# Setup of a two-layer mixer kernel: token tiles loaded first, scaled in pairs and turned row by row, zero products added, context work moved

## The chip, the cores and the metric

One core of one Trainium2 chip (trn2) runs the kernel, all in fp32. The metric is the device time of one execution in microseconds (us). The engines are TensorE (PE), VectorE (DVE), ScalarE (ACT), GpSimd (POOL) and SyncE (SP), which issues most DMAs. Before the change the median of 3 runs is 1315.41 us (1314.79 to 1315.99).

## The reference, cut to what matters

512 tokens `x` and 256 context rows `ctx` of 1024 features go through a first block (two gated linear-attention mixers) and then two attention layers. The change lies in the very first steps of the first block:

```python
mod_x = jnp.matmul(jax.nn.silu(c), w_mod[l]) + b_mod[l]
mod_c = jnp.matmul(jax.nn.silu(c_ctx), w_mod[l]) + b_mod[l]
...
hx = rmsnorm(x, norm_g[l]) * (1.0 + sc_x[:, None, :]) + sh_x[:, None, :]
hc = rmsnorm(ctx, norm_g[l]) * (1.0 + sc_c) + sh_c
z = jnp.matmul(h, w_in)        # queries, keys, values, gates, low-rank gate inputs
```

The relative-position bias (`rel_bias_2` against a one-hot table) is also turned into rows in the setup; the attention layers read them from DRAM much later.

## The kernel before

Each engine has one in-order program, written as functions `setup_t` (TensorE), `setup_v` (VectorE), `setup_a` (ACT), `setup_g` (POOL), `setup_s` (SP), followed by `gla_t`, `gla_v` and so on. There is no planner: the order on every engine is the order of the code, and engines meet through counting semaphores (`nt`, `nv`, `na`, `ng` hold the counts, `s_...` those of landings). `meet(e, "setup")` at the head of the `gla_*` functions waits for every engine's setup and for the bias rows' landing in DRAM (`s_br`).

The setup has these pieces. Tiles 2 to 5 of `xsv` are the tokens (128 rows of 1024 each), tiles 0 and 1 the context.

- SP (L294 to L314) issues in order: `c`, `c_ctx`, the identity (`cst`), 4 token tiles, 2 context tiles, two parts of `w_mod` (k = 0 and 2), the low-rank weights, the first half of the query and key weights (`s_aq`), then `w_mod` 1 and 3, the rest of the query weights, the constants, the weights of `load(s, 2)`, and, once ACT has written the bias rows, three stores to `bias_rows`. ACT's own queue (L485 to L489) loads small rows, `gdn_conv`, `rel_bias` and the one-hot table.
- ACT waits for `c` and `c_ctx`, does the silu (L492), then the squares with row sums of the six tiles in the order 2, 3, 4, 5, 0, 1 (L495). It later copies the bias rows and half of the turned tiles out of PSUM.
- VectorE copies `vec`, `cvec` and `rt` (L421 to L426) out of PSUM, makes the roots' arguments (`rsq_v`, L407), for which POOL takes the power of -0.5 (`rsq_g`, L412), and scales the tiles (L458, L462): all four token tiles after one root.
- TensorE turns the small rows (L320 to L324), makes the bias rows (`brow`, products of 33 rows by 13 columns), turns the tokens feature block by feature block, four row tiles each, so all four scaled tiles are needed for the first one (L353), does `mod(0)`, turns the context (L362), does `mod(2)`, and turns the two product rows into columns (`mod_turned`, products with 2 columns). `mod(k)` is 512 columns of the modulation matrix; from parts 0 and 2 come shift and scale of features 0 to 511 (`turned`, L443 to L446), from 1 and 3 those of features 512 to 1023.
- VectorE and ACT modulate the turned tiles in place in SBUF, `hT` for tokens, `hC` for context (L451, L453, L512, L514), the even ones on VectorE and the odd ones on ACT.
- TensorE then does `low_rank(t, 0)` on the first four feature tiles, and `mod(1)`, `mod(3)` and parts of the query products (`queries`) in turn. `gla_t` goes on with `low_rank(t, 1)`, `queries(t, 0, 4, 8)`, the products with `gla_up` (loaded at L601, after the meeting), `queries(t, 1, 4, 8)` and the keys (`key(0)`, `key(1)`). Nearly all products have line L147 (`mm`). An fp32 product is issued as two passes, so 8 of the trace's MATMULs of 512 columns are 4 products.

The products of the later stages wait for features through `t.wait_ge(...)` by parity of the tile; PSUM banks are handed out by `ps.take` from a ring or by number.

## Time and profile before

| | us |
|---|---|
| median of 3 runs | 1315.41 |
| profiled execution, span of its instructions | 1313.0 |
| what lies around the span, median less span | 2.4 |
| TensorE busy in the span | 1266.9 |
| VectorE / ACT / POOL busy | 698.7 / 417.0 / 398.1 |

How to read it: the span runs from the first instruction of the program to the last, of one execution that the profiler recorded; the time of the runs has a fixed part more, ahead and behind. The trace's times count from the span's start. An engine's busy time says how full it is over the whole span; what a change of one stage is worth has to be read from that stage.

### The profile page before, as it was taken

How to read it: one execution, taken by the hardware profiler on the slowest of the kernel's cores; microseconds unless marked ns; L12 is line 12 of the kernel's file. 1: busy time of each engine (PE TensorE's matmuls, PEld its weight loads, DVE VectorE, ACT ScalarE, POOL GpSimd, SP SyncE). 2: the span in 40 equal slices, each digit the busy share in tenths (PEclk: the TensorE clock that was granted, in tenths of full speed). 3: DMA queues.
4: the chain of work that ended last, by engine and by line, in shares of the span. 5: the costliest groups of instructions: out<-in, count | busy, mean ns of one | idle time of the engine just before them, and what ended most of it. 6: DMA issues, size and time to landing. Idle time of an engine off the chain costs nothing.

```text
span 1313.0 us, 24617 instructions
## 1 busy us (share of the span) xinstructions
PE 1266.9 (96%) x9971; PEld 772.5 (59%) x9971; DVE 698.7 (53%) x1422; ACT 417.0 (32%) x904; POOL 398.1 (30%) x470
## 2 busy tenths in 40 slices
PE   5999999999999999999999999999999999999997
PEld 3454655555656666687445885446645786455553
DVE  4356567847234444573473563247646373237745
ACT  4243213253433332101024002347613102236721
POOL 0100000202334443181432320225761250115671
PEclk9999999999999999999999999999999999999999
DMA  9710112011130100042426315110004415100001
GB/s 308 288 64 0 67 66 80 26 39 65 66 130 3 67 3 3 2 153 104 147 74 137 97 32 192 65 53 1 2 16 98 135 33 192 65 1 2 1 1 64
DMA packets 71535, 96.59 MB, mean 74 GB/s; under 512 B 27639, under 2 KB 35247, under 8 KB 71422
## 3 DMA queue, kind: packets, MB, share of 16 engines
q1 hardware_dynamic: 71050, 94.76, 21.7%
q8 instruction: 78, 1.28, 0.4%
q14 instruction: 35, 0.29, 0.1%
q10 hardware_dynamic: 372, 0.27, 0.1%
HBM read 92.89 MB, written 2.13 MB: 72 GB/s over the span
## 4 chain that ended last, share of the span: by engine, by line
PE 85%; DVE 6%; SPq 3%; ACT 3%; issue 1%; DMA 1%; POOL 0%; DVEq 0%; POOLq 0%; ACTq 0%
PE PS L147 81%; PE PS L2830 2%; DVE AR L2936 2%; ACT AR L3058 1%; SPq L187 1%; DMA bias_rows<-AR 1%; DVE AR L2923 1%; SPq L304 1%; SPq L308 1%; ACT AR L3068 0%; SPq L309 0%; SPq L312 0%; DVE AR L2106 0%; DVE AR L866 0%; PE PS L2164 0%
## 5 line engine op out<-in xcount | busy, mean ns | idle before, releaser
L147 PE MATMUL PS<-AR 64*64 64x64 f32 (+13 forms) x9334 | 1196.2, 326 | 21.8 <-ACT AR L3068 6.0
L147 PEld LDWEIGHTS PS<-AR 64*64 64x64 f32 (+5 forms) x9334 | 703.0, 152 | 485.1 <-issue 384.7
L3058 ACT ACTIVATE AR<-AR 128x257 f32<-128x257 f32 (+5 forms) x160 | 84.9, 531 | 96.1 <-DVE AR L2936 86.1
L2936 DVE CUSTOM_DVE_ANT_0 AR<-PS,AR 128x257 f32<-128x257 f32 (+5 forms) x160 | 72.2, 451 | 60.5 <-PE PS L147 43.0
L412 POOL TENSOR_TENSOR AR<-AR 128x1 f32<-128x1 f32 (+4 forms) x26 | 21.9, 841 | 258.6 <-DVE AR L407 211.8
L1189 DVE SCALAR_TENSOR_TENSOR AR<-AR 128x441 f32<-128x441 f32 (+2 forms) x96 | 78.6, 819 | 15.7 <-ACT AR L1146 12.0
L3119 POOL TENSOR_SCALAR AR<-AR 128x257 f32<-128x257 f32 (+5 forms) x96 | 53.4, 556 | 75.8 <-DVE AR L2942 70.3
L1612 DVE TENSOR_TENSOR AR<-PS,AR 128x256 f32<-128x256 f32 x60 | 25.5, 424 | 85.7 <-PE PS L147 82.4
L3117 POOL TENSOR_SCALAR AR<-AR 128x128 f32<-128x128 f32 (+3 forms) x64 | 39.0, 609 | 68.4 <-DVE AR L2942 64.5
L2053 POOL TENSOR_TENSOR AR<-AR 128x512 f32<-128x512 f32 x36 | 49.6, 1377 | 29.0 <-DMA AR<-in_w_o 26.0
L1738 ACT ACTIVATE AR<-PS 128x512 f32<-128x512 f32 x48 | 28.7, 597 | 82.5 <-PE PS L147 80.3
L2830 PE MATMUL PS<-AR 128*128 128x128 f32 x352 | 49.0, 278 | 4.5 <-DVE AR L2923 3.8
L2830 PEld LDWEIGHTS PS<-AR 128*128 128x128 f32 x352 | 38.6, 141 | 23.7 <-issue 12.4
L2106 DVE TENSOR_TENSOR AR<-PS,AR 128x512 f32<-128x512 f32 x40 | 27.7, 691 | 45.1 <-PE PS L147 43.3
L2372 POOL TENSOR_TENSOR AR<-AR 128x512 f32<-128x512 f32 x32 | 39.7, 1242 | 16.8 <-PE PS L147 13.9
L1850 POOL TENSOR_TENSOR AR<-AR 128x512 f32<-128x512 f32 x20 | 21.0, 1050 | 71.0 <-PE PS L147 62.4
L3068 ACT ACTIVATE AR<-PS 128x512 f32<-128x512 f32 (+2 forms) x56 | 30.0, 536 | 28.6 <-PE PS L2830 24.5
L2573 DVE SCALAR_TENSOR_TENSOR AR<-AR,PS 128x512 f32<-128x512 f32 x16 | 11.0, 687 | 52.0 <-ACT AR L2578 52.0
L2398 DVE SCALAR_TENSOR_TENSOR AR<-PS,AR 128x256 f32<-128x256 f32 x56 | 23.8, 424 | 25.8 <-PE PS L147 15.8
L3129 POOL TENSOR_TENSOR AR<-AR 128x28 f32<-128x28 f32 (+3 forms) x8 | 2.5, 315 | 99.9 <-DVE AR L2952 99.3
L1209 POOL TENSOR_TENSOR AR<-AR 128x512 f32<-128x512 f32 (+1 forms) x12 | 13.0, 1082 | 64.6 <-ACT AR L1155 46.4
L2923 DVE COPY AR<-PS 128x512 f32<-128x512 f32 (+2 forms) x48 | 28.9, 602 | 6.5 <-PE PS L2830 4.7
(264 smaller groups left out, 964.8 us busy)
## 6 DMA issues: line engine op xcount, KB each, us to landing
AR<-in_w_in SPq DMA_DIRECT2D x16, 2048.0 KB, 9.1
AR<-in_w_mod SPq DMA_DIRECT2D x6, 2048.0 KB, 13.1
AR<-in_w_out SPq DMA_DIRECT2D x4, 2048.0 KB, 13.0
AR<-in_x SPq DMA_DIRECT2D x8, 512.0 KB, 5.1
AR<-in_w_in SPq DMA_DIRECT2D x4, 1024.0 KB, 7.4
AR<-in_w_o SPq DMA_DIRECT2D x2, 2048.0 KB, 8.2
AR<-in_w_in SPq DMA_DIRECT2D x2, 1664.0 KB, 8.7
AR<-in_w_in SPq DMA_DIRECT2D x12, 256.0 KB, 4.2
```

The costliest lines, as they stand in the source:

```text
L147: return t.matmul(o, l, r, start=s, stop=p, skip_group_check=True)
L1189: v.do.scalar_tensor_tensor(out=o_, in0=xi[:, r0 + i - 1:r1 + i - 1, c0 + c - 1:c1 + c - 1], scalar=tap(i, c), in1=o_, op0=ALU.mult, op1=A ...
L1738: a_.do.activation(XX[n], ps.two("xx", n, k_, k)[:, new_at(k):new_at(k) + 512], ACT.Copy, bias=0.0, scale=1.0).then_inc(sa, na("xx", n, k_ ...
L2053: g.do.tensor_tensor(o, x, y, ALU.subtract).then_inc(sg, ng(*name, "T"))
L2372: g.do.tensor_tensor(o, x, y, op).then_inc(sg, ng("lS", l, p, i))
L2830: x = t.go.transpose(p[:, c + 128 * b:c + 128 * b + 128], PB[j % NJP][e][:, at[b]:at[b] + 128], ident)
L2923: write(dst, src).then_inc(sem, count("pT", l, j, e))
L2936: v.do.tensor_tensor_reduce(PB[j % NJP][e][:, 0:nk], ps["s", l, j, e][:, 0:nk], bias_for(qb, kind, 2 * a + e, nk), 1.0, 3e38, ALU.add, ALU ...
L3058: a_.do.activation(P, P, ACT.Exp, bias=mn[:, j % NJS, e:e + 1], scale=-1.0, accum_out=su[:, j % NJS, e:e + 1]).then_inc(sa, na("p", l, j, e))
L3068: out_of_psum(a_, sa, na, lambda o, x: a_.do.activation(o, x, ACT.Copy, bias=0.0, scale=1.0), l, i - TURN, e)
L3117: x = g.do.tensor_scalar(P, P, r, gt_[:, qb, c:c + 1], ALU.mult, ALU.mult)
L3119: x = g.do.tensor_scalar(P, P, r, one_c, ALU.mult, ALU.mult)
```

## The change

SP loads the token tiles ahead of `c`, `c_ctx` and the identity. POOL first clears a spare region `idle`, and TensorE runs 12 products of 256 columns on it (`kept_warm`) before anything else, and 6 more between `mod_turned(0)` and `mod(2)`. Roots of the tokens are taken for tiles 2 and 3, then for 4 and 5; VectorE scales tiles 2, 3 and 4, ACT tile 5. TensorE turns each tile as it comes (8 blocks in two banks); VectorE copies out its first half, ACT its second. The small copies `vec`, `cvec` and `rt` come behind these on VectorE, the squares of the context behind these on ACT. The bias rows move behind the token turns, `mod_turned(0)` ahead of `mod(2)`, the context turns behind `mod_turned(2)`, two tiles to a bank; the first context tiles are modulated straight out of PSUM, four are copied or modulated later, and the split between VectorE and ACT for `hC` goes by pairs. The first half of key tile 0 for the tokens (`key_of_tokens`) is done at the end of the setup, the second half in `gla_t`, whose ring of banks is 1 to 6. The core of the diff (the removed copies and the old order of the bias rows stand in the listing above):

```diff
+    idle = mrow[:, 1536:1792]
...
     def setup_s(s):
+        for i in range(4):
+            s.go.dma_start(xsv[:, 2 + i, :], I["x"][0, 128 * i:128 * i + 128, :]).then_inc(s_x[2 + i], 16)
         s.go.dma_start(cinv[:, :, 0], I["c"][0].rearrange("(p t) -> p t", t=8)).then_inc(s_c, 16)
         s.go.dma_start(cinv[:, :, 1], I["c_ctx"].rearrange("(p t) -> p t", t=8)).then_inc(s_c, 16)
         s.go.dma_start(cst[:, 0:C_TRI], I["consts"][:, 0:C_TRI]).then_inc(s_cst, 16)
-        for i in range(4):
-            s.go.dma_start(xsv[:, 2 + i, :], I["x"][0, 128 * i:128 * i + 128, :]).then_inc(s_x[2 + i], 16)
         for i in range(2):
...
+    def kept_warm(t, name, bank, n):
+        p = ps.take(t, "warm", name, bank=bank)
+        for i in range(n):
+            mm(t.go, p[:, 0:256], idle[:, 0:128], idle[:, 0:256], True, True)
     def setup_t(t):
+        t.wait_ge(sg, ng["idle"])
+        kept_warm(t, 0, 7, 12)
         t.wait_ge(s_cst, 16)
         t.wait_ge(s_rows, 16 * (len(ROWS) + 1))
-        p = ps.take(t, "vec")
+        p = ps.take(t, "vec", bank=6)
         t.go.transpose(p[:, 0:nrows], stage[0:nrows, 0:128], ident[0:nrows, 0:nrows])
         t.go.transpose(p[:, 128:236], stage2[0:108, 0:128], ident[0:108, 0:108]).then_inc(st, nt("vec"))
         t.wait_ge(s_rl, 16)
-        p = ps.take(t, "rl")
+        p = ps.take(t, "rl", bank=7)
...
         for a in range(4):
-            t.wait_ge(sv, nv["xn", 2 + a])
+            t.wait_ge(*((sa, na["xn", 5]) if a == 3 else (sv, nv["xn", 2 + a])))
+            for i in range(2):
+                p = ps.take(t, "hT", a, i, bank=(2 * a + i) % 6)
+                for m in range(4):
+                    x = t.go.transpose(p[:, 128 * m:128 * m + 128], xsv[:, 2 + a, 512 * i + 128 * m:512 * i + 128 * m + 128], ident)
+                x.then_inc(st, nt("hT", a, i))
+        t.wait_ge(s_oh, 32)
+        t.wait_ge(sv, nv["rt"])
+        for i, (k, lo, hi) in enumerate(BIAS):
+            p = ps.take(t, "brow", k, lo, bank=2 + i)
+            mm(t.go, p[0:13, 0:hi - lo], rt[0:33, 0:13], oh[0:33, 640 * k + lo:640 * k + hi], True, True).then_inc(st, nt("brow", k, lo))
+        t.wait_ge(sa, na["silu_c"])
+        mod(0)
+        mod_turned(0)
+        kept_warm(t, 1, 6, 6)
+        mod(2)
+        mod_turned(2)
+        for a in range(2):
+            t.wait_ge(sv, nv["xn", a])
         for m in range(8):
-            p = ps.take(t, "hT", m)
-            for a in range(4):
-                x = t.go.transpose(p[:, 128 * a:128 * a + 128], xsv[:, 2 + a, 128 * m:128 * m + 128], ident)
-            x.then_inc(st, nt("hT", m))
-        t.wait_ge(sa, na["silu_c"])
-        ps.ring = list(range(8))
-        mod(0)
-        t.wait_ge(sv, nv["xn", 1])
-        for m in range(8):
-            p = ps.take(t, "hC", m)
+            p = ps["hC", m // 2] if m % 2 else ps.take(t, "hC", m // 2, bank=4 + m // 2)
             for a in range(2):
-                x = t.go.transpose(p[:, 128 * a:128 * a + 128], xsv[:, a, 128 * m:128 * m + 128], ident)
-            x.then_inc(st, nt("hC", m))
-        mod(2)
-        mod_turned(0)
-        mod_turned(2)
+                x = t.go.transpose(p[:, 256 * (m % 2) + 128 * a:256 * (m % 2) + 128 * a + 128], xsv[:, a, 128 * m:128 * m + 128], ident)
+            if m % 2:
+                x.then_inc(st, nt("hC", m // 2))
         low_rank(t, 0)
+        queries(t, 0, 0, 4)
         mod(1)
-        queries(t, 0, 0, 4)
+        queries(t, 1, 0, 2)
         mod_turned(1)
+        queries(t, 1, 2, 3)
         mod(3)
-        queries(t, 1, 0, 2)
+        queries(t, 1, 3, 4)
         mod_turned(3)
-        queries(t, 1, 2, 4)
+        key_of_tokens(t, 0, 0, 4)
         nt.mark("at", "setup")
+    def features(t, h, t8):
+        by_scalar = t8 % 2 if h == "hT" else t8 // 2 % 2
+        t.wait_ge(*((sa, na[h, t8]) if by_scalar else (sv, nv[h, t8])))
...
+    def key_of_tokens(t, a, t0, t1):
+        w, = weights(t, 1) if t0 >= 4 else wviews(1)
+        t.wait_ge(s_aq, 16)
+        p = ps.banks[0] if t0 else ps.take(t, "ak", a, 256, bank=0)
+        for t8 in range(t0, t1):
+            features(t, "hT", t8)
+            x = mm(t.go, p[:, :], w[:, t8, 256 + 128 * a:384 + 128 * a], hT[:, t8, :], t8 == 0, t8 == 7)
+        if t1 == 8:
+            x.then_inc(st, nt("ak", a, 256))
...
+        def normed(row):
+            v.do.tensor_scalar(xsv[:, row, :], xsv[:, row, :], rstd[:, row:row + 1], None, ALU.mult).then_inc(sv, nv("xn", row))
+        def turned_tokens(a):
+            v.wait_ge(st, nt["hT", a, 0])
+            v.do.tensor_copy(hT[:, 0:4, 128 * a:128 * a + 128], ps["hT", a, 0].rearrange("p (m n) -> p m n", m=4)).then_inc(sv, nv())
+            ps.empty(sv, nv, "hT", a, 0)
+        v.wait_ge(sa, na["squares", 3])
+        rsq_v(v, rstd[:, 2:4], ss[:, 2:4], 1.0 / 1024, "x", 0)
+        normed(2)
+        normed(3)
+        v.wait_ge(sa, na["squares", 5])
+        rsq_v(v, rstd[:, 4:6], ss[:, 4:6], 1.0 / 1024, "x", 1)
+        turned_tokens(0)
+        normed(4)
+        for a in range(1, 4):
+            turned_tokens(a)
...
-        v.wait_ge(sa, na["squares", 5])
-        rsq_v(v, rstd[:, 2:6], ss[:, 2:6], 1.0 / 1024, "x")
-        for i in range(2, 6):
-            v.do.tensor_scalar(xsv[:, i, :], xsv[:, i, :], rstd[:, i:i + 1], None, ALU.mult).then_inc(sv, nv("xn", i))
         v.wait_ge(sa, na["squares", 1])
         rsq_v(v, rstd[:, 0:2], ss[:, 0:2], 1.0 / 1024, "ctx")
+        row(0)
         for i in range(2):
-            v.do.tensor_scalar(xsv[:, i, :], xsv[:, i, :], rstd[:, i:i + 1], None, ALU.mult).then_inc(sv, nv("xn", i))
-        for m in range(0, 8, 2):
-            v.wait_ge(st, nt["hT", m])
-            v.do.tensor_copy(hT[:, m, :], ps["hT", m][:, :]).then_inc(sv, nv())
-            ps.empty(sv, nv, "hT", m)
-        row(0)
-        for m in range(0, 8, 2):
-            v.wait_ge(st, nt["hC", m])
-            v.do.tensor_copy(hC[:, m, :], ps["hC", m][:, 0:256]).then_inc(sv, nv())
-            ps.empty(sv, nv, "hC", m)
+            normed(i)
+        turned(0)
         row(2)
-        turned(0)
         turned(2)
-        modulated(0)
+        for m in (0, 2):
+            v.do.tensor_scalar(hT[:, m, :], hT[:, m, :], modA[:, m:m + 1], modB[:, m:m + 1], ALU.mult, ALU.add).then_inc(sv, nv("hT", m))
+        v.wait_ge(st, nt["hC", 0])
+        for m in range(2):
+            v.do.tensor_scalar(hC[:, m, :], ps["hC", 0][:, 256 * m:256 * m + 256], modA[:, 8 + m:9 + m], modB[:, 8 + m:9 + m],
+                               ALU.mult, ALU.add).then_inc(sv, nv("hC", m))
+        ps.empty(sv, nv, "hC", 0)
+        v.wait_ge(st, nt["hC", 2])
+        v.do.tensor_copy(hC[:, 4:6, :], ps["hC", 2].rearrange("p (m n) -> p m n", m=2)).then_inc(sv, nv())
+        ps.empty(sv, nv, "hC", 2)
         row(1)
         turned(1)
         row(3)
         turned(3)
-        modulated(1)
+        v.wait_ge(sa, na["hT", "turned"])
+        for m in (4, 6):
+            v.do.tensor_scalar(hT[:, m, :], hT[:, m, :], modA[:, m:m + 1], modB[:, m:m + 1], ALU.mult, ALU.add).then_inc(sv, nv("hT", m))
+        for m in (4, 5):
+            v.do.tensor_scalar(hC[:, m, :], hC[:, m, :], modA[:, 8 + m:9 + m], modB[:, 8 + m:9 + m], ALU.mult, ALU.add).then_inc(sv, nv("hC", m))
         nv.mark("at", "setup")
...
+        def squares(i):
             a.wait_ge(s_x[i], 16)
             a.do.activation(junk, xsv[:, i, :], ACT.Square, bias=0.0, scale=1.0, accum_out=ss[:, i:i + 1]).then_inc(sa, na("squares", i))
+        for i in range(2, 6):
+            squares(i)
+        a.wait_ge(sg, ng["rsq", "x", 1])
+        a.do.activation(xsv[:, 5, :], xsv[:, 5, :], ACT.Copy, bias=0.0, scale=rstd[:, 5:6]).then_inc(sa, na("xn", 5))
+        for i in range(4):
+            a.wait_ge(st, nt["hT", i, 1])
+            a.do.activation(hT[:, 4:8, 128 * i:128 * i + 128], ps["hT", i, 1].rearrange("p (m n) -> p m n", m=4), ACT.Copy, bias=0.0, scale=1.0).then_inc(sa, na("hT", "turned"))
+            ps.empty(sa, na, "hT", i, 1)
+        for i in range(2):
+            squares(i)
...
-        for m in range(1, 8, 2):
-            a.wait_ge(st, nt["hT", m])
-            a.do.activation(hT[:, m, :], ps["hT", m][:, :], ACT.Copy, bias=0.0, scale=1.0).then_inc(sa, na())
-            ps.empty(sa, na, "hT", m)
-        for m in range(1, 8, 2):
-            a.wait_ge(st, nt["hC", m])
-            a.do.activation(hC[:, m, :], ps["hC", m][:, 0:256], ACT.Copy, bias=0.0, scale=1.0).then_inc(sa, na())
-            ps.empty(sa, na, "hC", m)
         for half in range(2):
             for k in (half, 2 + half):
                 a.wait_ge(sv, nv["modAB", k])
             for m in range(4 * half + 1, 4 * half + 4, 2):
                 a.do.activation(hT[:, m, :], hT[:, m, :], ACT.Identity, bias=modB[:, m:m + 1], scale=modA[:, m:m + 1]).then_inc(sa, na("hT", m))
-            for m in range(4 * half + 1, 4 * half + 4, 2):
-                a.do.activation(hC[:, m, :], hC[:, m, :], ACT.Identity, bias=modB[:, 8 + m:9 + m], scale=modA[:, 8 + m:9 + m]).then_inc(sa, na("hC", m))
+            if half == 0:
+                a.wait_ge(st, nt["hC", 1])
+            for m in (4 * half + 2, 4 * half + 3):
+                x = hC[:, m, :] if half else ps["hC", 1][:, 256 * (m % 2):256 * (m % 2) + 256]
+                a.do.activation(hC[:, m, :], x, ACT.Identity, bias=modB[:, 8 + m:9 + m], scale=modA[:, 8 + m:9 + m]).then_inc(sa, na("hC", m))
+            if half == 0:
+                ps.empty(sa, na, "hC", 1)
+                a.wait_ge(st, nt["hC", 3])
+                a.do.activation(hC[:, 6:8, :], ps["hC", 3].rearrange("p (m n) -> p m n", m=2), ACT.Copy, bias=0.0, scale=1.0).then_inc(sa, na())
+                ps.empty(sa, na, "hC", 3)
...
     def setup_g(g):
+        g.do.memset(idle, 0.0).then_inc(sg, ng("idle"))
         g.do.memset(mhalf_c, -0.5).then_inc(sg, ng())
         g.do.memset(rt[0:33, :], 0.0).then_inc(sg, ng())
         g.do.memset(rt[32:33, :], NEG).then_inc(sg, ng("rt"))
-        rsq_g(g, rstd[:, 2:6], "x")
+        rsq_g(g, rstd[:, 2:4], "x", 0)
+        rsq_g(g, rstd[:, 4:6], "x", 1)
         rsq_g(g, rstd[:, 0:2], "ctx")
...
-        ps.ring = list(range(7))
+        ps.ring = [1, 2, 3, 4, 5, 6]
         w, = weights(t, 1)
         def key(a):
             for lo, hi in XC:
+                if a == 0 and lo:
+                    key_of_tokens(t, 0, 4, 8)
+                    continue
```

## Rows read from the trace of the kernel before

**Rows 1.** page, part 1: engine, busy time, share, instructions
```profile
PE 1266.9 (96%) x9971; PEld 772.5 (59%) x9971; DVE 698.7 (53%) x1422; ACT 417.0 (32%) x904; POOL 398.1 (30%) x470
```

**Rows 2.** busy time by stretch: PE, PEld, DVE, ACT, POOL, clock, DMA share, GB/s
```profile
18.00:21.00 3.00, 2.60 (x13) 2.63 (x14) 1.94 (x5) 1.09 (x3) 0.70 (x1) 1.00 1.05 387
...
32.90:36.50 3.60, 3.59 (x9) 2.07 (x11) 1.27 (x3) 2.19 (x4) 0.00 (x0) 0.54 1.05 389
```

**Rows 3.** timeline, TensorE: start, us, instruction, count, wait before it
```profile
13.35 4.44 PE L147 MATMUL PS<-AR 33*13 33x512 f32 x8 [1.78 <-DMA AR<-in_onehot]
18.41 5.89 PE L353 MATMUL PS<-AR 128*128 128x128 f32 x32 [0.62 <-DVE AR L458]
24.22 1.93 PE L147 MATMUL PS<-AR 128*32 128x512 f32 x16
...
27.97 3.80 PE L147 MATMUL PS<-AR 128*32 128x512 f32 x32
...
32.91 23.75 PE L147 MATMUL PS<-AR 128*64 128x512 f32 x104 [1.14 <-DVE AR L451]
...
37.55 0.16 PEld L147 LDWEIGHTS PS<-AR 128*32 128x32 f32 x8 [0.39 <-DMA AR<-in_w_mod]
...
56.83 33.48 PE L147 MATMUL PS<-AR 128*128 128x512 f32 x106 [0.18 <-DMA AR<-in_gla_up]
```

**Rows 4.** timeline, ACT, to 13 us
```profile
7.26 0.22 ACT L492 ACTIVATE AR<-AR 128x16 f32<-128x16 f32 x1
7.57 1.06 ACT L495 ACTIVATE AR<-AR 128x1024 f32<-128x1024 f32 x1
...
8.81 1.06 ACT L495 ACTIVATE AR<-AR 128x1024 f32<-128x1024 f32 x1
...
12.65 1.06 ACT L495 ACTIVATE AR<-AR 128x1024 f32<-128x1024 f32 x1 [1.31 <-DMA AR<-in_x]
```

**Rows 5.** timeline, VectorE and POOL, 11 to 34 us
```profile
11.47 0.24 DVE L421 COPY AR<-PS 128x76 f32<-128x76 f32 x1 [9.98 <-PE PS L321]
...
12.15 0.16 DVE L426 COPY AR<-PS 32x12 f32<-32x12 f32 x1
...
15.13 3.12 DVE L458 TENSOR_SCALAR AR<-AR 128x1024 f32<-128x1024 f32 x4 [1.14 <-POOL AR L412]
...
18.61 0.70 POOL L412 TENSOR_TENSOR AR<-AR 128x2 f32<-128x2 f32 x1 [3.51 <-DVE AR L407]
...
32.22 1.13 DVE L451 TENSOR_SCALAR AR<-AR 128x512 f32<-128x512 f32 x2
```

**Rows 6.** timeline, SP's queue: start and time of each issue
```profile
2.91 1.86 SPq L298 DMA_DIRECT2D AR<-in_x  x4
4.81 1.02 SPq L300 DMA_DIRECT2D AR<-in_ctx  x2
...
37.26 5.91 SPq L312 DMA_DIRECT2D bias_rows<-AR  x1
```

**Rows 7.** DMA issues, us to landing; then lines L298, L300 and L304 (first two)
```profile
AR<-in_c_ctx SPq DMA_DIRECT2D x1, 4.0 KB, 3.1
...
DMA to landing us min/median/max: 3.9/5.6/8.3
...
DMA to landing us min/median/max: 9.3/9.6/10.0
...
DMA to landing us min/median/max: 14.9/17.4/19.8
```

**Rows 8.** TensorE: one line's durations (ns); products of 256 columns, 60 to 90 us
```profile
L353 PE MATMUL PS<-AR x32: 272/421/445, 18.4 to 24.0; 128*128 128x128 f32 x32
...
L147 PE MATMUL PS<-AR 128*128 128x256 f32 x36 | 8.4, 378 | 0.0
```

**Rows 9.** timeline, VectorE, 104 to 109 us
```profile
104.25 0.96 DVE L848 TENSOR_TENSOR AR<-AR 128x768 f32<-128x768 f32 x1 [0.91 <-ACT AR L972]
108.38 0.69 DVE L750 COPY AR<-PS 128x512 f32<-128x512 f32 x1 [3.17 <-PE PS L147]
```

More of the change, by code:

```diff
@@ L342, in mod_turned @@
             t.wait_ge(sv, nv["mrow", k])
-            p = ps.take(t, "modT", k, bank=2 + k // 2 if k % 2 else None)
+            p = ps.take(t, "modT", k, bank=2 + k // 2)
             for m in range(4):
@@ L387, in low_rank @@
                     t8 = 2 * i + q
-                    t.wait_ge(*((sa, na[h, t8]) if t8 % 2 else (sv, nv[h, t8])))
+                    features(t, h, t8)
                     x = mm(t.go, p[64 * q:64 * q + 64, 0:hi - lo], w[:, t8, :], hx[:, t8, :], i == 0, i == 3)
@@ L546, in projT @@
         for t8 in range(8):
-            t.wait_ge(*((sa, na[h, t8]) if t8 % 2 else (sv, nv[h, t8])))
+            features(t, h, t8)
             x = mm(t.go, p[0:m, 0:hi - lo], w[:, t8, c:c + m], hx[:, t8, :], t8 == 0, t8 == 7)
```

17 lines of the change are left out of this document (2 added, 15 removed).

## The prediction, written before the result was known

> **What bounds the kernel now.** I read the page first: TensorE is busy 1266.9 of 1313.0 us [rows 1]. The table by stage shows it full from 33 us on, though at a granted clock of 0.54 between 32.9 and 36.5, that is mostly at 1.2 instead of 2.4 GHz [rows 2]. So a setup edit is worth what it moves the point from which TensorE has no more holes. TensorE's timeline gives the pieces [rows 3]: small work before 13.35, then the bias rows, the token turns from 18.41, mod(0) 24.22, context turns, mod(2) 27.97, then 1.14 us of waiting for VectorE, low_rank(0) at 32.91, mod(1) at 37.55. After that one packed stretch runs to 56.83, with a hole of 0.18. The chain that leads to 18.41 is ACT's silu and squares, VectorE's and POOL's reciprocal roots and VectorE's scaling [rows 4, 5]. I call the start of mod(2) M and of ACT's first square s. Before, M is 27.97 and s is 7.57.
>
> **DMA queues.** SP issues c, c_ctx and the identity first, then four token tiles from 2.91 and two context tiles from 4.81 [rows 6]. Landings follow the order of issue: a context tile takes 9.6 us because the tokens are ahead of it, the last token tile 8.3 us, the first 3.9 [rows 7]. The change puts the token loads ahead of c and c_ctx, but ACT's order stays: it still waits for both c's, does the silu, and only then the squares. So everything of ACT is now queued behind c_ctx. The first tile, issued at about 0.72 (the time of the first load now, 2.19 ahead of 2.91), lands after 3.9 at 4.6. The stream gives 387 GB/s between 18 and 21 us [rows 2], which is 1.3 us a tile of 524 kB, so the fourth is there at 8.6 to 9.6 (the small row loads of ACT's queue share the engines; in the trace the fourth came at 12.6, 5.8 us after the first, not 4) [rows 4]. c_ctx took 3.1 us for 4 kB in a nearly empty queue [rows 7], mostly latency; in a full one I bound both c's together by 0.5 and 2 us (estimate). c_ctx lands between 9.1 and 11.6; I take 10.3. The silu is done 0.3 us after its start [rows 4], so s = 10.7, bounds 9.4 and 12. The tokens themselves no longer limit the squares. Before, the square of the last tile waited 1.31 us for its load [rows 4]; that wait goes, but s moves by +3.1.
>
> In a sentence of its own: the Trainium skill (DMA: Bandwidth & Descriptors, section on queues, rings and completion order) says that on each DMA engine descriptors are consumed in ring order, while completion across engines is not in order; by the first half c waits as I have it, by the second it could not overtake by more than one engine's lag. The trace's landings agree with the first.
>
> **The token part.** A square and its sum take 1.24 us from one to the next (7.57 to 8.81) [rows 4]. The second one is ready at s+2.4. Root: VectorE 0.17 and POOL 0.70 for two columns (the row of 18.61; with four it was 1.02) with gaps, 1.0 together [rows 5]. Scaling is 0.78 a tile (3.12 for 4). First pair: tile 2 at s+4.2, tile 3 at s+5.0. Before, the pairs were one group of four, and TensorE waited for the last; now it starts after the first tile: s+4.35. Second root on POOL to s+5.95; ACT scales tile 5 in 1.06, to s+7.1; VectorE first copies out half of tile 2's turns (0.69) and then scales tile 4, to s+7.5. TensorE needs it at s+7.8 at the earliest, if it turns 16 blocks at the low clock, so it isn't held. 32 turns took 5.89 us [rows 3], and their durations, 421 ns in the median and 272 at least, show both clocks [rows 8]: 128 columns at intervals of 0.21 and 0.11 us, the change coming at about 22.9. All low would be 6.8, all high 3.4. I take 5.8, the row itself, since TensorE again comes out of idle: last turn at s+10.15.
>
> **The bias rows** wait on VectorE, which now copies vec, cvec and rt after the fourth half tile. Last first-half turn s+9.7, latency 0.3, copy 0.69, the three copies 0.84 (11.47 to 12.31) [rows 5]: TensorE can go on at s+11.6, a new hole of 1.4. The products took 4.44 at the low clock [rows 3], so 2.2 at the high: s+13.8. Then mod(0); its row's copy ends 2.7 after its start (26.90 against 24.22) and mod_turned(0) starts at s+16.65 and takes 0.9 (the piece at 27.97 is 3.80, of which mod(2) is 1.9 as mod(0) was, and 16 two-column products the rest) [rows 3]. Then six zero products, 12 passes of 256 columns at 0.22 (36 such passes 8.4 us, with ends) [rows 8]: 2.6 us. They would fill a wait for w_mod[2], but that has landed at 26.3 (issued 6.5, 19.8) [rows 7], and with s = 10.7 TensorE gets there at 28.2. So they lie on the path. M = s+20.15 = 30.85.
>
> **From mod(2) to the packed stretch.** Before, low_rank(0) began at M+4.94: 1.99 to VectorE's copy of the row, 0.69, turned products, two small VectorE operations, the first modulation 0.57 (1.13 for two) [rows 5]. Now mod_turned(0) is out of the way, but the context turns, 16 at 0.11 with 0.1 of start, come in behind mod_turned(2), which ends at M+3.7. So low_rank(0) starts at M+5.5; the first modulated tiles are ready at M+4.8. Its four context features come by VectorE at M+6.3 and by ACT at M+7.2 (0.57 and 0.83 us a token tile, 0.43 and 0.61 a context tile), as they are wanted: no hole. low_rank(0) took 4.64 (32.91 to 37.55) [rows 3], of which 3.6 were at the low clock; at the high one it is 2.7. Everything after it was at M+9.58 and is at M+8.15: the change gains 1.43 here, mostly the low clock of 32.9 to 36.5 [rows 2]. That counts on the context turns keeping TensorE busy where it had 1.14 us of nothing after the 2-column products.
>
> Behind it stand the same products. key_of_tokens(0,0,4), 3.4 us, is work taken from later, so it costs or gives nothing unless a wait is ahead of it. The gla_up wait (0.18 at 56.83 [rows 3]) disappears: bias rows go out at 37.26 on SP whatever ACT does, since SP is held by its own loads until then [rows 6]. Twelve zero products at the start, 24 passes, run from 1.2 to between 6.4 and 11.5, before anything else of TensorE can run. The chain of the gates' softplus starts with the u products, at about 61.6 instead of 56.83. The keys' end factors of head pair 0 were ready at 105.2, and TensorE came for them at 108.4 (VectorE had waited 3.17 us for it) [rows 9]. If all of the 4.8 goes through, they come at 110.0 and TensorE at 109.7: a stall between 0 and 0.3, and I take 0.
>
> Sum: (30.85 - 27.97) - 1.43 = +1.45 us, less the 0.2 of the gla_up wait: +1.25. Against the span that is 1314.3; the median of the runs stands 2.4 above the span, so 1316.7.
>
> **Rivals.**
> 1. c is not held by the tokens (it needed 3.1 us after issue for c_ctx [rows 7]). Then ACT's table load sets s = 7.5 as now, M = 27.7 and the sum is -1.9: 1313.5. For it: the c's are 4 kB each. Against it: the order of landings. 14%.
> 2. The zero products hold the clock until the tokens come. The turns show 0.21 us each until TensorE had turned blocks for 4.5 us, then 0.11 [rows 3, 8]. If it is high from the start, the turns take 3.4 and end as fast as VectorE and ACT feed them: 2.4 saved, 1314.3 with s = 10.7. Together with rival 1, M cannot be before w_mod[2] at 26.3: -3.1 - 0.2, 1312.1. But with s = 10.7 TensorE's turns start at 15, several us after the zeros end. 8% alone, 7% with rival 1. The Trainium skill (TensorE: Matmul & The Clock Gate, Part 1) says that the low clock is the default and activity lifts it; by it these products buy nothing if idle time follows.
> 3. Slower: the clock falls again. The 1.4 us hole ahead of the bias rows, which only use 33 rows and 13 columns, resembles the stretch ahead of 32.9 (1.14 us of nothing) after which the clock was low. If it does, the bias rows take up to 4.4, mod(0) or the zero products a part of 1.2 more: +2 to +3.5, 1318.7 to 1320.2. It decides if idle time and light products meet. The same place holds a late c_ctx (s = 12: +1.3). 20%.
>
> **How the numbers follow.** Likeliest, 51%: 1316.7, on its own from 1315.4 (s = 9.4) to 1318.0 (s = 12). About 0.2% (2.6 us) can be told from no change. Faster than 1312.8: rivals 1 and 2 together, and a small part of rival 1, 0.11. Slower than 1318.0: rival 3 and the upper edge of the forecast, 0.29. Range: 1313.3 to 1319.5.
>
> **What would show it.** ACT's silu starting at 10.3 instead of 7.26, for a wait on c_ctx; first token turn at 15.1; turns of 0.21 us; a hole of 1.4 before the bias rows, released by VectorE's rt copy; six zero products right before mod(2) with w_mod[2] already there; low_rank(0) at 36 and clock 1.00 there. I am wrong if silu starts near 7.3, if mod(2) waits for its load, or if the packed stretch has new holes after 60.

## The result, and the profile after

The changed kernel took 1320.6 us (median of six runs, 1320.38 to 1327.22), beside 1314.7 us for the kernel before on the same chip (six runs, the three of the table among them). The ratio is 1.0058, with an interval from 1.0048 to 1.0067: **slower by 0.6%**, 3.9 us above the forecast of 1316.7 and above its range.

One run of all those below was slow through its whole length (2109.75 us at a granted clock of 0.574, in e3) and is counted nowhere. The six times of the changed kernel are not one heap. Four lie between 1320.38 and 1320.65, at granted clocks of 0.994 to 0.995 over the whole run, and two at 1326.99 and 1327.22, at 0.989 and 0.991. I call them the lower and the upper group. The profile that came with the result is of the upper group; a repeat of the same kernel (e12 below) gave one of the lower (1321.31 us, span 1319.5), and that is the one to set against the sum. First lines of the page of the repeat:

```profile
span 1319.5 us, 24682 instructions
...
PE 1274.2 (97%) x10007; PEld 779.3 (59%) x10007; DVE 698.2 (53%) x1419; ACT 417.4 (32%) x902; POOL 399.2 (30%) x472
```

TensorE is busy 7.3 us more than before [rows 1]. That says little of the 6.5 us of span: the zero products at the start alone are 8.14 us, and they stand where TensorE had been idle. The timeline of TensorE in the repeat, against [rows 3] (start, us, instruction, count, wait before it):

```profile
1.08 8.14 PE L147 MATMUL PS<-AR 128*128 128x256 f32 x24 [1.08 <-POOL AR L570]
...
15.54 5.98 PE L355 MATMUL PS<-AR 128*128 128x128 f32 x32 [3.83 <-DVE AR L448]
22.72 4.17 PE L147 MATMUL PS<-AR 33*13 33x512 f32 x24 [1.21 <-DVE AR L472]
27.75 5.61 PE L147 MATMUL PS<-AR 128*128 128x2 f32 x36 [0.87 <-DVE AR L479]
34.18 1.05 PE L147 MATMUL PS<-AR 128*128 128x2 f32 x8 [0.81 <-DVE AR L479]
35.09 1.95 PE L373 MATMUL PS<-AR 128*128 128x128 f32 x16
...
38.19 32.02 PE L147 MATMUL PS<-AR 128*64 128x512 f32 x140 [1.15 <-DVE AR L507]
```

A row merges neighbours of one line and names the first shape. The row of 22.72 is the eight bias-row products and the sixteen of mod(0). The row of 27.75 is mod_turned(0), twelve zero passes and mod(2), which by its 1.93 us [rows 3] began at 31.44: that is M. low_rank(0) starts at 38.19, M+6.75. ACT in the same trace, against [rows 4]:

```profile
11.00 0.22 ACT L533 ACTIVATE AR<-AR 128x16 f32<-128x16 f32 x1 [3.26 <-DMA AR<-in_c_ctx]
11.31 1.06 ACT L536 ACTIVATE AR<-AR 128x1024 f32<-128x1024 f32 x1
```

So ACT stood 3.26 us with its table loaded, for a load of 4 kB, and s is 11.31. To follow the rest of the run I took the same VectorE instruction, counted from the last one, in both traces. The changed kernel is late by 3.25 us at 135 us, by 4.0 at 815, by 5.9 at 822, by 6.1 at 1120 and by 6.5 at the end. **Half of the loss arises in the setup, half in stages that the diff hardly touches.** The setup was forecast at +1.25, the later stages at nothing. TensorE between 811 and 822 us, first in the kernel before:

```profile
808.12 10.91 PE L147 MATMUL PS<-AR 128*128 128x512 f32 x28
819.42 2.06 PE L147 MATMUL PS<-AR 128*128 128x64 f32 x9 [0.39 <-DVE AR L2936]
```

And in the repeat of the changed one, 4.0 us later:

```profile
812.14 7.05 PE L147 MATMUL PS<-AR 128*128 128x512 f32 x16
820.87 4.10 PE L147 MATMUL PS<-AR 128*128 128x512 f32 x12 [1.68 <-DVE AR L2630]
```

The same 28 passes are now in two parts, with 1.68 us of nothing between them. TensorE writes its products into the eight banks of PSUM that `ps.take` hands out, and the program makes it wait until the last reader of a bank is done. Line 2630 is the output gate's last use of such a bank: a product waits for a bank, not for data. No such wait was there before.

The upper group's trace has the same holes, and something more. TensorE's timeline in the profile that came with the result:

```profile
16.13 6.67 PE L355 MATMUL PS<-AR 128*128 128x128 f32 x32 [3.77 <-DVE AR L448]
24.01 6.42 PE L147 MATMUL PS<-AR 33*13 33x512 f32 x24 [1.21 <-DVE AR L472]
31.29 7.83 PE L147 MATMUL PS<-AR 128*128 128x2 f32 x36 [0.87 <-DVE AR L479]
```

Its windows (stretch, TensorE's busy time, granted clock, DMA share, GB/s):

```profile
22.30:25.60 3.30, 2.09 (x11) 1.00 1.10 353
25.70:29.10 3.40, 3.40 (x15) 0.50 0.87 214
29.10:32.40 3.30, 2.43 (x14) 0.50 1.05 401
...
35.90:39.00 3.10, 3.10 (x23) 1.00 1.04 384
```

And those of the repeat:

```profile
13.40:20.20 6.80, 4.67 (x22) 0.50 1.05 391
20.30:24.90 4.60, 3.39 (x19) 1.00 1.13 338
25.00:37.00 12.00, 10.32 (x77) 1.00 1.02 367
```

In the repeat the clock is at 2.4 GHz from 20.3 on and stays there. In the other it rose at 22.3, with the turns all but done, and from 25.7, in the products behind the hole of 1.21 us, it is at 1.2 GHz again until 35.9. The bias rows with mod(0) take 6.42 instead of 4.17, the next row 7.83 instead of 5.61, and M is at 37.19. That is 5.75 later than in the repeat: 0.59 from s, 0.7 from slower turns and the rest from the second low stretch. At 135 us this run is late by 9.0, at the end by 12.2, so the later stages lose 3.2 in both. The parts differ a little: 0.6 of the upper run's 3.2 is one more stretch at a granted clock of 0.50, from 1193.1 to 1199.8, that the repeat doesn't have.

### The profile page after: what moved, and what is told of

The parts are those of the page before. It is cut to its first block, busy times and chain, and to the rows that moved or that the text cites. A ratio compares the mean times of both kernels' runs of the same rounds, so it can differ in the third digit from the quotient of the medians.

```text
span 1325.2 us, 24682 instructions
## 1 busy us (share of the span) xinstructions
PE 1280.9 (97%) x10007; PEld 783.4 (59%) x10007; DVE 699.5 (53%) x1419; ACT 417.1 (31%) x902; POOL 398.6 (30%) x472
## 3 DMA queue, kind: packets, MB, share of 16 engines
q1 hardware_dynamic: 71050, 94.76, 21.5%
## 4 chain that ended last, share of the span: by engine, by line
PE 87%; DVE 6%; ACT 3%; issue 1%; DMA 1%; SPq 0%; POOL 0%; DVEq 0%; POOLq 0%; ACTq 0%
PE PS L147 83%; PE PS L2887 3%; DVE AR L2993 1%; ACT AR L3115 1%; DMA AR<-in_c_ctx 1%; DMA AR<-in_final_g 1%; DVE AR L2980 1%; PE PS L355 0%; ACT AR L3125 0%; DVE AR L923 0%; PE PS L2221 0%; DVE AR L2163 0%; POOL AR L439 0%; ACT AR L1785 0%; DVE AR L2128 0%
## 5 line engine op out<-in xcount | busy, mean ns | idle before, releaser
L147 PE MATMUL PS<-AR 64*64 64x64 f32 (+11 forms) x9370 | 1208.8, 327 | 24.8 <-ACT AR L3125 4.8
L147 PEld LDWEIGHTS PS<-AR 64*64 64x64 f32 (+4 forms) x9370 | 712.4, 152 | 491.8 <-issue 388.2
L439 POOL TENSOR_TENSOR AR<-AR 128x1 f32<-128x1 f32 (+3 forms) x27 | 22.2, 824 | 263.0 <-DVE AR L434 216.2
L1246 DVE SCALAR_TENSOR_TENSOR AR<-AR 128x441 f32<-128x441 f32 (+2 forms) x96 | 78.7, 819 | 15.8 <-ACT AR L1203 11.7
```

Of the source, the lines that this page charges most:

```text
L147: return t.matmul(o, l, r, start=s, stop=p, skip_group_check=True)
L1246: v.do.scalar_tensor_tensor(out=o_, in0=xi[:, r0 + i - 1:r1 + i - 1, c0 + c - 1:c1 + c - 1], scalar=tap(i, c), in1=o_, op0=ALU.mult, op1=A ...
```

## The experiments

Each is the changed kernel with an edit, unless said otherwise, and each computes everything of the reference. Zero products, where an edit takes them out, feed nothing. "Before" is the kernel before on the same chip: 1314.5 us beside e1 to e4, 1315.0 beside e5 to e8, 1314.5 beside e9 to e12. These three sets ran on different chips, so small differences from one set to another are to be read through the kernel before.

**e1: the silu behind the four token squares.** If s hangs on c_ctx, ACT should do the squares first.

```
-        a.wait_ge(s_c, 32)
-        a.wait_ge(sv, nv["csv"])
-        a.do.activation(csv[:, :, 0:2], cinv, ACT.Silu, ...)
...
         for i in range(2, 6):
             squares(i)
+        a.wait_ge(s_c, 32)
+        a.wait_ge(sv, nv["csv"])
+        a.do.activation(csv[:, :, 0:2], cinv, ACT.Silu, ...)
```

> The changed kernel with ACT's silu (and its wait for c and c_ctx) moved behind the four token squares; everything else as changed. In the changed kernel's trace the silu waits until 11.59 for c_ctx, and the squares start at 11.90. Theory (ACT is held by c_ctx, queued behind the tokens): the squares start when ACT's table load ends, at about 8.9, the first token turn moves from 16.1 to about 13.1, and the time falls by 3.0 us, from 1320.6 to 1317.6. Rival (the setup is lost to the low clock alone, whose periods do not move with ACT): squares start earlier but mod(2) starts within 1 us of where it did, and the time stays within 1 us of 1320.6. A rival of the other kind: the earlier start makes the low-clock stretches fall elsewhere, then the gain is 0 to 6 us.

Measured: 1318.5 us (ten runs), beside 1314.5; ratio 1.0033 (1.0021 to 1.0044). ACT's first square and TensorE's first turn in its trace:

```profile
7.92 1.06 ACT L533 ACTIVATE AR<-AR 128x1024 f32<-128x1024 f32 x1
12.15 5.33 PE L355 MATMUL PS<-AR 128*128 128x128 f32 x32 [0.58 <-DVE AR L448]
```

s fell by 3.4 and the first turn with it; M is 27.47, 4.0 less. In the profiled executions the gain is 4.4 (1319.5 to 1315.1), but that sets the slowest run of the lower group beside the second fastest of e1; in the medians it is 2.1, below the 3.0 that I expected. Nine runs spread from 1316.7 to 1320.8, and one at 1324.6 shows that the upper group stays. The wait for the queued c_ctx was the cause of the late s.

**e2: no zero products ahead of mod(2).** They lie on the path, or they keep the clock.

```
         mod_turned(0)
-        kept_warm(t, 1, 6, 6)
         mod(2)
```

> The changed kernel without the 6 zero products between mod_turned(0) and mod(2). w_mod[2] has landed at 26.4, long before TensorE gets there at 33. Theory (they lie on the path): mod(2) starts 2.6 us (high clock) to 4.2 us (as in the profiled run, mostly low clock) earlier, and the time falls by 2.6 to 3.5 us, to 1317.1 to 1318.0. Rival (they lift the clock, so that mod(2), the context turns and low_rank(0) run high): without them these three (1.9 + 1.7 + 2.7 us at the high clock) run at the low clock in whole or in part, and the time falls by less than 1 us or rises.

Measured: ratio 1.0065 (1.0045 to 1.0085), median 1324.5 of eight runs, in two groups: 1318.6, 1318.7 and 1319.0 at granted clocks of 0.994 to 0.995, and 1323.9 to 1327.6 at 0.985 to 0.988. Without them the lower group is 1.9 us faster (1318.7 against 1320.6), less than the 2.6 of the sum, and M comes 2.7 earlier in the trace (28.75). But five of eight runs fall into the upper group, against three of eleven with them (six runs of the result, five of e12), or nine of 40 when e1, e3, e5 and e11 are counted too. The row where they stood has 24 passes instead of 36:

```profile
27.77 2.91 PE L147 MATMUL PS<-AR 128*128 128x2 f32 x24 [0.87 <-DVE AR L478]
```

Both theories are partly right: the zero products lie on the path, and without them more runs may lose the clock. With so few runs the difference of the shares is a sign, not proof.

**e3: other banks for the context tiles.** The wait of 1.15 us before low_rank(0) is for VectorE's line 507, which empties the bank of context pair 0; low_rank(0) takes bank 4, the same one.

```
-            p = ... ps.take(t, "hC", m // 2, bank=4 + m // 2)
+            p = ... ps.take(t, "hC", m // 2, bank=(0, 1, 6, 7)[m // 2])
```

> The changed kernel with the four pairs of context turns in PSUM banks 0, 1, 6, 7 instead of 4, 5, 6, 7. In the changed kernel low_rank(0) waits 1.15 us for VectorE's modulation of context tiles 0 and 1 out of bank 4, although it begins with token tiles. Theory (it waits for the bank, not for a feature): the wait falls to under 0.3 us and the time by 0.8 to 1.1 us, to 1319.6. Rival (it waits for its features, or the wait reappears at the context part of low_rank(0)): the hole is as long or moves 1.7 us on, and the time stays within 0.3 us of 1320.6.

Measured: two runs of 1319.35 and 1319.53 and two of 1326.4, so the groups must be compared: 1319.4 against the changed kernel's 1320.6, 1.2 less. The ratio, 1.0073 (1.0049 to 1.0098), is of the four together, a mixture, and says little. The hole is gone:

```profile
34.87 1.94 PE L373 MATMUL PS<-AR 128*128 128x128 f32 x16
36.74 9.79 PE L147 MATMUL PS<-AR 128*64 128x512 f32 x43
```

With M at 31.21, low_rank(0) comes at M+5.53, where the prediction had M+5.5. The hole was a bank, not a late feature.

**e4: VectorE's small copies first.** vec, cvec, rt and the two small operations behind them move from behind the four half tiles to ahead of the first root; the hole before the bias rows should go.

```
+        v.wait_ge(st, nt["vec"])
+        v.do.tensor_copy(vec, p[:, 0:nrows]).then_inc(sv, nv())
...
         v.wait_ge(sa, na["squares", 3])
         rsq_v(v, rstd[:, 2:4], ss[:, 2:4], 1.0 / 1024, "x", 0)
```

> The changed kernel with VectorE's small copies (vec, cvec, rt, and the two small operations behind them) ahead of the roots, where they were before the change; the bias rows stay behind the token turns. Their inputs are there at 12.3 and VectorE is idle until 14.3. Theory (the hole of 1.2 us ahead of the bias rows waits for rt and the clock falls because of it): the hole goes, the bias rows follow the turns at once, the clock stays at 2.4 GHz through mod(0), mod_turned(0) and the zeros, and mod(2) starts 4 to 6 us earlier in a profile like the changed kernel's; the time falls by 2.5 to 5 us, to 1315.6 to 1318. Rival (the light products of 33 rows and 2 columns make the clock fall with or without the hole): the time falls by 1.2 us or less, to 1319.4, and the low stretch from about 26 is still there.

Measured: 1320.6 us (four runs, 1319.5 to 1322.4), ratio 1.0048 (1.0033 to 1.0063). The hole is gone:

```profile
15.59 6.59 PE L355 MATMUL PS<-AR 128*128 128x128 f32 x32 [3.06 <-DVE AR L448]
22.11 4.18 PE L147 MATMUL PS<-AR 33*13 33x512 f32 x24
```

The bias rows come 0.61 earlier than in the repeat, not 1.21, because the turns took 6.59 instead of 5.98: the clock rose only at 21.5. The median did not move. The expected 2.5 to 5 us didn't come. None of the four runs was in the upper group, but with eight of eleven runs in the lower group four in a row would lie there by chance in 28% of cases, so these four don't show that the hole is what lets the clock fall.

**e5: the later stages on the banks that they had.** PSUM banks without a fixed number are handed out from a ring by a running counter. The change gives fixed banks to the turns and mods, so the counter is lower when the setup ends: 12 instead of 35 at the end of the keys.

```
         ps.ring = list(range(8))
+        ps.k = 35
```

> The changed kernel with one line more: at the end of the keys in gla_t the counter of the PSUM ring is set to the value that it had there before the change (35, where the changed kernel has 12), so that every later stage takes the banks that it took before the change. Seen in the traces: TensorE's later waits have moved. The profile of the kernel before has no wait of over 1 us after 95 us, all five of the changed kernel's family have one of 1.68 us at about 820, released by VectorE's update of the output (line 2630), and one of 1.0 to 1.3 us at about 1220. Theory (the takes with a fixed bank no longer advance the counter, so later tiles fall on banks that are still being read): both holes go, and the time falls by 2.5 to 3 us, from 1320.6 to 1317.8, whatever the setup does. Rival (these holes come from the later phase of DMAs or of the clock): they stay, and so does the time, within 0.5 us.

Measured: 1318.4 us (ten runs; eight between 1317.4 and 1318.7, two at 1325), beside 1315.0; ratio 1.0035 (1.0021 to 1.0049). From 1320.6 to 1318.4 is 2.2 us. Lower groups alone, each counted above the kernel before on its chip, are 5.8 and 3.1 us above it, so the gain is 2.7. The profiled execution was of the upper group (late by 9.3 at 135 us), but its later stages lose only 0.6 more, against 3.2. The 28 passes that were in two parts now run from 818.03 without a wait; the rows show their last 20 and what follows:

```profile
821.48 7.46 PE L147 MATMUL PS<-AR 128*128 128x512 f32 x20
829.32 0.96 PE L147 MATMUL PS<-AR 128*128 128x64 f32 x5 [0.38 <-DVE AR L2994]
```

I had expected a second hole, near 1220 us, to go as well. It didn't: TensorE waits 1.34 us there for VectorE in the repeat and 1.34 in e5, where the kernel before has 0.98.

**e6: the kernel before, with the counter shifted.** One line on the kernel before, at the same place, and nothing of the change.

```
         ps.ring = list(range(8))
+        ps.k = 12
```

> The kernel before, with nothing of the change but the ring's counter: at the same place it is set to 12, the changed kernel's value, instead of 35. Theory: the holes at about 815 and 1217 appear in the kernel before, the setup's part of the trace stays as it is, and the time rises by 2.5 to 3 us, from 1314.6 to 1317.3. Rival: no hole, and the time within 0.3 us of 1314.6.

Measured: 1317.1 us (ten runs, 1316.8 to 1318.0), beside 1315.0; ratio 1.0019 (1.0009 to 1.0029). The hole appears in a kernel whose setup is untouched:

```profile
807.94 7.05 PE L147 MATMUL PS<-AR 128*128 128x512 f32 x16
816.67 4.10 PE L147 MATMUL PS<-AR 128*128 128x512 f32 x12 [1.68 <-DVE AR L2574]
```

In the profiles the shifted kernel is 0.3 us ahead of the kernel before at 135 us and 2.2 behind at the end: 1.9 lost at 817, 0.5 between 900 and 970, 2.5 in all. The wait near 1220 us stays at 0.98. So e5 and e6 together show it from both sides: 2.1 to 2.7 us of the loss in the medians, 2.5 and 2.6 in the profiles, are the counter, and the longer wait near 1220 us is not.

**e7: all four mends.** e1, e3, e4 and e5 in one kernel, zero products kept.

```
(the edits of e1, e3, e4 and e5)
```

> The changed kernel with four amendments together: silu behind the token squares, small copies of VectorE ahead of the roots, context turns in banks 0, 1, 6, 7, ring counter as before. Theory: the turns start at 12.2 and end at about 18, the bias rows follow without a hole, mod(0) waits for w_mod[0] at 20.9, the zeros still lie on the path, mod(2) starts at 27.2 (27.97 before) and low_rank(0) 5.5 us later; with the ring's 2.8 us taken back the time is 1312.3, that is 2.3 us under the kernel before. If the clock falls in the setup in some runs, these lie 3 to 6 us higher. Rival (the late holes do not come from the ring, or the idle wait for w_mod[0] drops the clock every time): 1315 to 1318.

Measured: 1316.5 us (ten runs, 1315.4 to 1317.1), ratio 1.0010 (1.0001 to 1.0019). All runs lie in one group, but the time is 4.2 above what I expected. The first turn came at 15.68, hardly earlier than in the repeat, although s was no longer held by c_ctx: VectorE now waits for the small transposes before the first root, and these need the identity, which lands behind the tokens. Two mends collide. e4's trace has this wait, harmless there since s was later. VectorE's first rows in e4:

```profile
12.44 0.24 DVE L457 COPY AR<-PS 128x76 f32<-128x76 f32 x1 [10.95 <-PE PS L329]
...
13.79 0.17 DVE L434 TENSOR_SCALAR AR<-AR 128x2 f32<-128x2 f32 x1
```

**e8: e7 without the zero products ahead of mod(2).**

```
(the edits of e7, and)
-        kept_warm(t, 1, 6, 6)
```

> As e7_all_mended, without the 6 zero products between mod_turned(0) and mod(2). Theory by the durations alone: mod(2) starts when w_mod[2] lands, at 26.4, and the time is 1311.5. Rival (the zeros' use is the clock: without them more runs have mod(2) to low_rank(0) at 1.2 GHz, as the spread of e2_no_zeros_between, 1318.6 to 1327.6 in 8 runs, hints): the median lies above that of e7_all_mended, at 1314 or more, and the runs spread over 5 us.

Measured: 1313.2 us (ten runs, 1311.9 to 1315.7), ratio 0.9988 (0.9978 to 0.9997), and 3.3 less than e7. TensorE:

```profile
14.83 5.41 PE L355 MATMUL PS<-AR 128*128 128x128 f32 x32 [3.07 <-DVE AR L447]
20.17 4.18 PE L147 MATMUL PS<-AR 33*13 33x512 f32 x24
25.21 2.91 PE L147 MATMUL PS<-AR 128*128 128x2 f32 x24 [0.87 <-DVE AR L478]
...
31.72 10.44 PE L147 MATMUL PS<-AR 128*64 128x512 f32 x47
```

The time is 1.7 above the 1311.5 of the durations alone. With the hole ahead of the bias rows and the one ahead of low_rank(0) gone, no run of ten is in an upper group though the zero products are out, against five of eight in e2. If they protect anything, it is only a path that has such a hole.

**e9: the small copies behind tile 4.** VectorE does them after scaling tile 4 and before the remaining three half tiles: behind the first root, ahead of the bias rows. Otherwise e8.

```
         normed(4)
-        for a in range(1, 4):
-            turned_tokens(a)
         v.wait_ge(st, nt["vec"])
...
+        for a in range(1, 4):
+            turned_tokens(a)
         def row(k):
```

> As e8_all_mended_no_zeros, but VectorE's small copies stand behind its scaling of tile 4 instead of ahead of the first root. In e8's trace they hold the first root from 10.4 to 13.0, because their inputs wait on TensorE for the identity, so the first turn is at 14.8; where they stood last (e1) it was at 12.15. w_mod[2] landed at 24.8 there. Theory: first turn at 12.2, no hole ahead of the bias rows, mod(2) at 24.8 to 25.2 instead of 26.2, time 1311.9 against 1313.2 of e8. Rival (the clock rises later relative to the turns, which eats the gain; or mod(2) waits for its load longer than in e8): 1313 or more.

Measured: 1312.2 us (ten runs, 1310.5 to 1315.4), beside 1314.5; ratio 0.9986 (0.9976 to 0.9995), **2.3 us faster than the kernel before**, and the best of the study, by 0.5 us over e8 (1.8), which the intervals don't separate. TensorE:

```profile
11.87 2.69 PE L355 MATMUL PS<-AR 128*128 128x128 f32 x16
15.24 3.67 PE L355 MATMUL PS<-AR 128*128 128x128 f32 x16 [0.67 <-DVE AR L447]
18.84 4.62 PE L147 MATMUL PS<-AR 33*13 33x512 f32 x24
24.33 2.91 PE L147 MATMUL PS<-AR 128*128 128x2 f32 x24 [0.87 <-DVE AR L478]
...
30.84 11.54 PE L147 MATMUL PS<-AR 128*64 128x512 f32 x53
```

The turns start 3.7 us earlier than in the repeat, and M is 25.31. But of the 2.96 us by which they start earlier than in e8 only 0.9 arrives at low_rank(0). TensorE waits 0.67 for tile 4, which VectorE scales behind the second root and the first half tile; the small copies stand behind it and hold nothing there. The rest went to the clock: from 14.6 to 19.7 it is 0.50, so that the turns take 6.36 instead of 5.41 and the bias rows with mod(0) 4.62 instead of 4.18.

**e10: e9 without any zero products.** The twelve at the start go too.

```
(the edits of e9, and)
-        t.wait_ge(sg, ng["idle"])
-        kept_warm(t, 0, 7, 12)
```

> As e9_copies_behind_tile4, without the 12 zero products at the start either. In all traces so far they lift the clock at about 5 and end at 8.4; it falls again at 11 to 13.5, about when the turns start, and the turns run at 1.2 GHz. Theory (they end too early to help): the turns start and end as in e9, the time within 0.7 us of e9. Rival (they keep the clock up into the first turns, or shift the moment at which it rises): 1.5 us or more slower than e9, the turns all at 0.21 us apart.

Measured: 1312.3 us (ten runs, 1310.7 to 1316.4), ratio 0.9985 (0.9975 to 0.9995): the same as e9. A new limit shows:

```profile
17.41 4.17 PE L147 MATMUL PS<-AR 33*13 33x512 f32 x24
24.79 3.59 PE L147 MATMUL PS<-AR 128*32 128x512 f32 x16 [1.24 <-DMA AR<-in_w_mod]
31.99 14.45 PE L147 MATMUL PS<-AR 128*64 128x512 f32 x71
```

TensorE reached mod(2) 1.24 us before its weights had landed, and mod(2) ran at 1.2 GHz (3.59 us instead of 1.93). The bias rows started 1.43 us earlier than in e9, and the load and the clock took it back. Why they started earlier is worth noting, since I expected the turns to end alike: from 14.6 to 19.7 us the granted clock is 1.00 in this trace, with 33 instructions of TensorE, and 0.50 in e9's, with 18, though the turns began at 11.98 and 11.87. In these two profiles the zero products at the start did not merely end too early; the clock rose later with them than without. The windows, e9's first:

```profile
14.60:19.70 5.10, 4.46 (x18) 0.50 1.05 388
14.60:19.70 5.10, 4.83 (x33) 1.00 1.05 391
```

**e11: the changed kernel without the zero products at the start.**

```
-        t.wait_ge(sg, ng["idle"])
-        kept_warm(t, 0, 7, 12)
```

> The changed kernel without the 12 zero products at the start. There the first turn is at 15 to 16, 7 us after the zeros end. Theory: no effect on the turns, time within 1 us of the changed kernel on the same chip, in its two groups (1320.5 and 1327 so far). Rival: slower by 2 us or more in the lower group.

Measured: 1320.1 us (1319.7, 1319.8, 1320.1, 1320.3 and 1327.3), ratio 1.0053 (1.0033 to 1.0074). Beside 1320.6 and 1320.9 with them, they gain nothing that can be measured.

**e12: the changed kernel again**, with no edit.

```
(no edit)
```

> The changed kernel itself once more, for its spread: 6 runs lay at 1320.4 to 1320.7 (4) and 1327.1 (2). If the groups are the clock's low stretch from about 26 on, caught or not, the granted clock of each run goes with its time: about 0.995 at 1320.5, 0.989 to 0.991 at 1327; a profile of the lower group shows no low stretch between 23 and 36, mod(2) at about 31 to 33, and the holes at 820 and 1220 in both.

Measured: 1320.9 us (1320.4, 1320.6, 1320.9, 1321.3 and 1327.9), ratio 1.0059 (1.0039 to 1.0079). Its profile is the repeat read above.

## Why the prediction was wrong

**The step that failed: "Behind it stand the same products".** By that sentence the stages after the setup were put at 0, but for a wait of 0 to 0.3 at the gates and 0.2 for gla_up. They lost 3.2 us, the largest error and enough by itself to leave the range (1319.9 against 1319.5). The products are the same, their PSUM banks are not: the diff puts a fixed bank at the turns, mods and transposes, and each such take no longer moves the counter from which all later stages get theirs. e6 shows the effect without the change and e5 the change without the effect. It stood in the diff, in `bank=` and in the new ring of the keys, and in none of the rows that I read. Of the 3.2, the profiles put 2.6 down to the counter (3.24 less the 0.6 left in e5) and 2.5 by e6; the medians say 2.1 to 2.7. The other 0.6 remained in e9 too (4.1 gained at 135 us, 3.4 at the end). Of it 0.36 is the wait near 1220 us, 1.34 instead of 0.98 in the repeat, e5 and e9, but 0.98 in e6: something else in the change lengthens it, and what is open. The remainder wasn't followed.

**s, forecast 10.7, was 11.31.** The mechanism was right: c_ctx behind four token tiles, silu behind c_ctx, squares behind the silu; e1 shows it. The term that was mis-sized is c_ctx's landing, taken at 10.3 and found near 11.0, 7.6 us after its issue in the repeat and 8.2 in the other profile, against 3.1 in [rows 7]. It lies inside the bounds (12 at most). Price +0.6. The issues themselves took long too; SP's queue in the profile of the result:

```profile
0.72 1.85 SPq L295 DMA_DIRECT2D AR<-in_x  x4
...
3.34 1.29 SPq L297 DMA_DIRECT2D AR<-in_c_ctx  x1
4.68 4.79 SPq L298 DMA_DIRECT2D AR<-in_consts  x1
```

The identity's issue took 4.79 us, so the context tiles were issued only from 9.5. It cost nothing here, as the context is now late by intent. The identity itself landed 7.1 us after its issue began (6.4 in the repeat, 7.4 in e7), and that is what held e7.

**From s to M, forecast s+20.15, was s+20.13** in the lower group. Piece by piece: first turn s+4.23 (4.35), turns 5.98 (5.8), hole 1.21 (1.4), the products of bias rows and mod(0) 4.17 (2.2 and 1.93), the zeros as priced. That the sum is right to 0.02 is in part luck, as turns 0.2 too short and a hole 0.2 too long cancel. The turns' row was a fair guide since TensorE again came out of idle.

**From M to the packed stretch: "no hole" was wrong by 1.15 us.** The features were there; VectorE in the repeat:

```profile
35.68 1.13 DVE L504 TENSOR_SCALAR AR<-AR 128x512 f32<-128x512 f32 x2
36.92 1.12 DVE L507 TENSOR_SCALAR AR<-PS,AR 128x256 f32<-128x256 f32 x2
38.15 0.69 DVE L511 COPY AR<-PS 128x512 f32<-128x512 f32 x1
```

Of the two token features of line 504 the first was ready near 36.2 (half of the row), M+4.8 as I had it, and the second at 36.8. low_rank(0) starts when line 507 ends, since it takes the bank that 507 reads. I asked which features each product wants and never which bank it takes. With it, the point after low_rank(0) is at M+9.45 (6.75 and 2.7) instead of M+8.15, and the gain of 1.43 is 0.13. e3 shows M+5.53 with another bank.

The sum, corrected: +1.25, +0.6 for c_ctx, +1.3 for the bank of low_rank(0), +3.2 for the later stages make +6.35; the repeat's span is +6.5. One term hid a part of the miss: I put the runs 2.4 above the span, a median of three against the span of one, where the repeat's own time is 1.8 above its span (1321.3 and 1319.5), as is that of the profile that came with the result.

**Rival 3** (the clock falls ahead of the bias rows, 20%) was right in its mechanism for the upper group only, 3 runs of 11, and its price was too low: 2.25 us on the bias rows with mod(0) and 2.22 on the row behind them, 4.47 together, where I had given it 2 to 3.5. The low stretch went on through mod_turned(0) and the zero products. What decides between the groups stays open. The repeat has the same hole and the same light products and kept its clock. Counted over all experiments, the upper group has 14 of the 48 runs that have the hole ahead of the bias rows (the result, e1, e2, e3, e5, e11, e12) and none of the 44 that don't (e4, e7 to e10). Three of the four edits of e7 were also run alone and kept upper runs (e1, e3, e5), which points to the fourth, the hole; the hole ahead of low_rank(0) comes after the fall at 25.7 and can't have caused it. That makes the hole ahead of the bias rows likely as a condition, not proven: the fourth edit alone, e4, has only four runs. Nor do e9 and e10 lie in one heap: three runs at 1314.7 to 1315.4 and two at 1314.8 and 1316.4 are 2.6 to 4.1 us above their medians, and no profile of one was taken.

**Rival 1** (c not held) was false: the silu waited 3.26 us. **Rival 2** (the first zeros hold the clock until the tokens come) was false too. They did lift it, but it had fallen again before the first turn. Windows of the repeat over the zero products:

```profile
5.00:7.00 2.00, 2.00 (x7) 1.00 1.03 404
7.00:9.00 2.00, 2.00 (x11) 1.00 1.07 212
```

They end at 9.22, and but for the three small transposes at 11.2 to 11.7 TensorE is idle until the first turn at 15.54. The window from 13.40 above is at 1.2 GHz. The Trainium skill (TensorE: Matmul & The Clock Gate, Part 1) has the low clock as the default and activity as what lifts it; by that rule products followed by idle time buy nothing, and e11 agrees: 1320.1 without them, 1320.6 and 1320.9 with them. e9 and e10 add that they can put the rise of the clock in the turns off.

**The middle zeros cost about what was said:** 2.6 was forecast; e2 shows 2.7 at M and 1.9 in its lower group, e8 against e7 3.3. That w_mod[2] had landed when TensorE came was right too: it never was the last to come until e10.

## What to carry to other kernels

When a change fixes or frees a buffer in one stage, write down which buffers every later stage gets from the shared counter, before and after: here that cost 2 to 3 us, most of it 800 us away from the edit. A line that sets the counter to its old value tests it. Before moving large loads ahead of small ones, list what each engine does first and for which load it waits; a 4 kB load cost 3 us of ACT, and doing the squares first gave them back. For a product that is to start early, check both of its waits, its operands and its bank.
